# First norm of an MLA and differential-attention trunk: input split on arrival, root applied to the latents

## The reference

```python
def rmsnorm(x, g, eps=NORM_EPS):
    xf = x.astype(jnp.float32)
    y = xf * lax.rsqrt(jnp.mean(xf * xf, axis=-1, keepdims=True) + eps)
    return (y * g.astype(jnp.float32)).astype(x.dtype)

h = rmsnorm(x, g_attn_pre[0])
lat = h @ w_down                                   # 1024 x 704
c_q = rmsnorm(lat[..., :384], g_q_lat)
c_kv = rmsnorm(lat[..., 384:640], g_kv_lat)
k_pe = rope(lat[..., 640:], cos, sin)
q = c_q @ w_uq
kv = c_kv @ w_ukv
```

## Time and profile before

| what | value |
| --- | --- |
| median of 3 runs | 2650.4 us (2642.67 to 2661.89) |
| the profiled execution's own time | 2648.62 us |
| its span in the profile | 2646.8 us |
| mean granted TensorE clock | 0.975 |
| TensorE busy in the span | 2455.5 us (93%) |

### The profile page before, as it was taken

One profiled execution on the slowest core, in us unless ns is written; L12 is line 12 of the kernel. 1 busy time (PEld: TensorE's weight loads), 2 busy tenths in 40 slices (PEclk: granted clock), 3 DMA queues, 4 the chain that ended last, 5 costly groups with the idle time before them and its releaser, 6 DMA issues.

```text
span 2646.8 us, 31568 instructions
## 1 busy us (share of the span) xinstructions
PE 2455.5 (93%) x11940; PEld 1962.3 (74%) x11940; DVE 1928.3 (73%) x2189; ACT 847.8 (32%) x1439; POOL 1478.9 (56%) x1133
## 2 busy tenths in 40 slices
PE   7999999999999999996799899988989999999994
PEld 4788888777777777773577787766777777777772
DVE  4467664696887888889766677763796878888878
ACT  3245442342111111113346555652342111111112
POOL 4231113635888888884431323213636888888883
PEclk9999999999999999998999999988999999999997
DMA  3121215411111111113211212142311111111112
GB/s 136 48 70 66 80 56 209 142 56 40 49 64 48 48 49 55 50 40 152 64 50 47 64 49 92 37 159 111 135 56 40 62 51 48 48 51 53 56 58 109
DMA packets 51237, 191.98 MB, mean 73 GB/s; under 512 B 5904, under 2 KB 6416, under 8 KB 47376
## 3 DMA queue, kind: packets, MB, share of 16 engines
q1 hardware_dynamic: 39184, 148.92, 16.8%
q10 hardware_dynamic: 11904, 41.05, 4.1%
HBM read 146.43 MB, written 29.36 MB: 66 GB/s over the span
## 4 chain that ended last, share of the span: by engine, by line
PE 73%; DVE 16%; ACT 5%; issue 3%; DMA 2%; SPq 1%; ACTq 0%; POOL 0%; POOLq 0%; DVEq 0%
PE ps L1187 9%; PE ps L1188 9%; PE ps L1189 9%; PE ps L1209 6%; PE ps L1210 5%; PE ps L1211 5%; PE ps L1018 3%; PE ps L990 2%; PE ps L992 2%; PE ps L991 2%; PE ps L1055 2%; PE ps L1110 1%; PE ps L1035 1%; PE ps L1112 1%; PE ps L1111 1%
## 5 line engine op out<-in xcount | busy, mean ns | idle before, releaser
L2026 DVE TENSOR_TENSOR a<-a,ps 128x1024 f32<-128x1024 f32 x336 | 409.1, 1219 | 195.1 <-PE ps L1211 187.5
L739 POOL CAST w_hi<-w_raw 128x1024 fp32r<-128x1024 f32 x78 | 84.8, 1087 | 774.1 <-PE ps L992 272.4
L1209 PE MATMUL ps<-hid,ring 128*128 128x512 f32 x704 | 295.9, 420 | 26.5 <-DVE a L2026 13.2
L1545 ACT ACTIVATE cy<-cx,cv 128x1024 f32<-128x1024 f32 x76 | 94.8, 1247 | 674.0 <-DVE cx L1997 674.0
L821 POOL TENSOR_TENSOR ring<-w_raw,ring 128x512 fp32r<-128x512 f32 x206 | 298.8, 1450 | 16.5
L1210 PE MATMUL ps<-hid,ring 128*128 128x512 f32 x704 | 278.5, 396 | 0.0
L1211 PE MATMUL ps<-hid,ring 128*128 128x512 f32 x704 | 277.9, 395 | 0.0
L819 POOL CAST ring<-w_raw 128x512 fp32r<-128x512 f32 x206 | 168.2, 816 | 182.8 <-PE ps L1211 91.9
L1187 PE MATMUL ps<-h,ring 128*128 128x512 f32 x608 | 236.7, 389 | 0.0
L1188 PE MATMUL ps<-h,ring 128*128 128x512 f32 x608 | 236.7, 389 | 0.0
L1189 PE MATMUL ps<-h,ring 128*128 128x512 f32 x608 | 236.5, 389 | 0.0
(11 more groups left out here) (263 smaller groups left out, 6532.9 us busy)
## 6 DMA issues: line engine op xcount, KB each, us to landing
w_raw<-in_W SPq DMA_DIRECT2D x166, 512.0 KB, 3.2
raw_d<-in_W SPq DMA_DIRECT2D x44, 512.0 KB, 3.2
h<-o_dram ACTq DMA_DIRECT2D x2, 6144.0 KB, 20.7
x_dram<-x ACTq DMA_DIRECT2D x6, 2048.0 KB, 8.2
x<-x_dram SPq DMA_DIRECT2D x2, 4096.0 KB, 12.7
dsw<-draw SPq DMA_DIRECT2D x64, 128.0 KB, 2.3
o_dram<-most SPq DMA_DIRECT2D x6, 1024.0 KB, 4.0
o_dram<-dost SPq DMA_DIRECT2D x6, 1024.0 KB, 3.9
```

Of the source, the lines that this page charges most:

```text
L1209: pe.matmul(out, wh, xh, start=True, stop=False)
L2026: dve.tensor_tensor(a[:, f, :], a[:, f, :], src, ALU.add).then_inc(acc_done, 1)
```

## The change

- The four DMAs of the input's first half and the one of `par` change places in ACT's queue: `par` is first.
- In the first norm ACT rounds the input times its factor per channel straight into `h` (a Copy with the factor as its scale), then squares the input into a buffer of its own for each tile (`xs0`, `xs1`, `xs2`; no wait for TensorE). DVE computes input times factor minus the rounded part into `h` in one operation. The root is not in `h` any more.
- DVE adds the squares of k = 0 to 6 of each half, six additions, in PSUM bank 4; the last of them writes to SBUF. TensorE then sums a half with two matmuls by ones (`first_sums`): half 0 behind the first two turns of the first pair, half 1 behind its last turn. The 16 matmuls of `x_stats(0)` are gone.
- The root of each half is made by ACT from banks 6 and 7 into `rstd_0`. DVE multiplies each latent bank by it where it used to copy the bank.
- POOL has no part in the first norm.
- DVE's last three operations on lambda stand behind `latents()`.

```diff
--- before.py
+++ after.py
@@ -418,6 +418,8 @@
         assert off[0] <= base + 51 * SLOT + small_cols * 4
         cst = at("cst", 22, 1)
         lam_raw = nc.alloc_sbuf_tensor_at("lam_raw", [P, 256], F32, offset=base + 23 * SLOT)
+        xs0, xs1, xs2 = at("xs0", 38, 4), at("xs1", 42, 3), at("xs2", 28, 1)
+        rstd_0 = at("rstd_0", 45, 1)
         lam_mul = nc.alloc_sbuf_tensor_at("lam_mul", [P, 128], F32, offset=base + 24 * SLOT)
 
         ps = ctx.enter_context(nc.psum_tensor("ps", [P, 8 * HB], F32))
@@ -446,6 +448,7 @@
         a_sq, ss_add, a_stat, a_ln, a_rstd = (sem(n) for n in ("a_sq", "ss_add", "a_stat", "a_ln", "a_rstd"))
         a_normed, x_sq, x_stat, x_ln, x_rstd = (sem(n) for n in (
             "a_normed", "x_sq", "x_stat", "x_ln", "x_rstd"))
+        x0_hi, x0_lo, x0_add, x0_stat = (sem(n) for n in ("x0_hi", "x0_lo", "x0_add", "x0_stat"))
         f_new, b_kept, acc_first, xq_add, b_stat = (sem(n) for n in (
             "f_new", "b_kept", "acc_first", "xq_add", "b_stat"))
         h_f, h_hi = sem("h_f"), sem("h_hi")
@@ -487,7 +490,7 @@
         N_T = HEADS * NJ * (NJ + 1) // 2
         X_IN = {1: 16, 2: 32, 3: 48, 4: 64}
         SPILLED = {1: 16, 2: 32, 3: 48}
-        H_NO = {0: 0, 2: 1}
+        H_NO = {2: 0}
         X_NO = {2: 0, 4: 1}
 
         SQ0 = {"wo0": 0, "ffn0": 2 * KT - 1, "wo1": 3 * KT - 1, "ffn1": 5 * KT - 2}
@@ -552,6 +555,12 @@
         def added_bank(half):
 
             return bank((5, 1)[half])
+
+        def first_squares(half, k):
+
+            if half == 0:
+                return half_of(xs0, k // 2, k % 2)
+            return half_of(xs1, k // 2, k % 2) if k < 6 else half_of(xs2, 0, k - 6)
 
         def squares_of(half, k):
 
@@ -852,7 +861,6 @@
             pool.memset(ones[:, :], 1.0).then_inc(consts_ready, 1)
             for u in range(2):
                 split(u, u)
-            norm_help(0, sums=False)
             for u, free in enumerate(pairs_free(0, 0, by_half=True)):
                 split(u, 2 + u, free)
             with pool.Fori(2, LT // 2) as q:
@@ -895,8 +903,20 @@
                 pe.matmul(bank(6 + half), ones[:, :], squares_of(half, KT - 1), start=False, stop=True
                           ).then_inc(b_stat, 1)
 
+            def first_sums(half):
+
+                pe.wait_ge(x0_add, (KT - 2) * (half + 1))
+                pe.matmul(bank(6 + half), ones[:, :], first_squares(half, KT - 2), start=True, stop=False
+                          ).then_inc(x0_stat, 1)
+                pe.wait_ge(x_sq, KT * (half + 1))
+                pe.matmul(bank(6 + half), ones[:, :], first_squares(half, KT - 1), start=False, stop=True
+                          ).then_inc(x0_stat, 1)
+
             def wait_h(n, half, k):
-                wait_norm(pe, h_lo, H_NO[n], half * KT + k)
+                if n == 0:
+                    pe.wait_ge(x0_lo, half * KT + k + 1)
+                else:
+                    wait_norm(pe, h_lo, H_NO[n], half * KT + k)
 
             def pair_of_units(unit, ch, first_bank_use, norm, by_half=False, between=None):
 
@@ -930,7 +950,8 @@
                                   start=t == t0, stop=t == t1 - 1).then_inc(l_stat, 1)
 
             def latents():
-                pair_of_units(0, 0, True, 0, by_half=True)
+                pair_of_units(0, 0, True, 0, by_half=True, between=lambda: first_sums(0))
+                first_sums(1)
                 pair_of_units(2, 4, False, None)
 
                 pair_of_units(4, 8, False, None, between=lambda: latent_stats(0, QT, 4))
@@ -1223,7 +1244,6 @@
 
 
             pe.wait_ge(consts_ready, 1)
-            x_stats(0)
             latents()
 
             pe.wait_ge(consts_in, 16)
@@ -1263,21 +1283,31 @@
                 act.wait_ge(dn_done, down_count(layer, n - 2, KT - 1))
                 act.activation(cx[:, 2 * (n % 2), 0:HB], up_bank(n, "P1"), ACT.Copy).then_inc(bank_copied, 1)
 
-            def x_norm(n, first=False, spill=False):
+            def first_norm():
+
+                act.wait_ge(par_in, 16)
+                for i, (half, k) in enumerate(NORM_TILES):
+                    if k % 2 == 0:
+                        act.wait_ge(x_part[4 * half + k // 2], 16)
+                    act.activation(half_of(h, 2 * k, half), half_of(x, k, half), ACT.Copy, scale=gain("attn_pre0", k)
+                                   ).then_inc(x0_hi, 1)
+                    act.activation(first_squares(half, k), half_of(x, k, half), ACT.Square).then_inc(x_sq, 1)
+                for half in range(2):
+                    act.wait_ge(x0_stat, 2 * half + 2)
+                    rstd(half_of(rstd_0, 0, half), bank(6 + half), D, 0, x_ln, half + 1, x_rstd)
+
+            def x_norm(n, spill=False):
                 for step, i in NORM_STEPS:
                     if step == "L":
-                        act.wait_ge(x_stat, n // 2 * 16 + (i + 1) * KT)
+                        act.wait_ge(x_stat, (i + 1) * KT)
                         rstd(half_of(rstd_x, 0, i), bank(6 + i), D, 0, x_ln, 2 * n + i + 1, x_rstd)
                         continue
                     half, k = NORM_TILES[i]
                     if step == "A":
-                        if first:
-                            act.wait_ge(x_part[4 * half + k // 2], 16)
-                        else:
-                            wait_norm(act, x_new, X_NO[n], i)
+                        wait_norm(act, x_new, X_NO[n], i)
                         if i >= 2:
 
-                            act.wait_ge(x_stat, n // 2 * 16 + i - 1)
+                            act.wait_ge(x_stat, i - 1)
                         act.activation(half_of(sq, 0, i % 2), half_of(x, k, half), ACT.Square).then_inc(x_sq, 1)
                         if spill and k == KT - 1:
 
@@ -1619,8 +1649,8 @@
                     act.dma_start(x[:, 2 * g:2 * g + 2, half * HB:(half + 1) * HB],
                                   x_first[:, 2 * g:2 * g + 2, half * HB:(half + 1) * HB]).then_inc(x_part[4 * half + g], 16)
 
+            act.dma_start(par[:, :], small).then_inc(par_in, 16)
             load_x(0)
-            act.dma_start(par[:, :], small).then_inc(par_in, 16)
             load_x(1)
             act.dma_start(ident[:, :], consts[:, 0:128]).then_inc(consts_in, 16)
             act.dma_start(cst[:, 0, 0:512], consts[:, 128:640]).then_inc(mask_in, 16)
@@ -1633,7 +1663,7 @@
             act.wait_ge(eps_set, 2)
 
             act.preload_act_table_set("natural_log_exp_and_others")
-            x_norm(0, first=True)
+            first_norm()
 
             act.wait_ge(lam_step, 2)
             act.activation(lamb[:, 2:4], lamb[:, 0:2], ACT.Exp).then_inc(lam_exp, 1)
@@ -1661,6 +1691,26 @@
 
         @block.vector
         def _(dve):
+            def first_norm():
+
+                def add_square(i):
+                    half, k = NORM_TILES[i]
+                    if not 1 <= k <= KT - 2:
+                        return
+                    dve.wait_ge(x_sq, i + 1)
+                    dve.wait_ge(x0_add, (KT - 2) * half + k - 1)
+                    dve.tensor_tensor(first_squares(half, k) if k == KT - 2 else bank(4),
+                                      first_squares(half, 0) if k == 1 else bank(4), first_squares(half, k), ALU.add
+                                      ).then_inc(x0_add, 1)
+
+                for i, (half, k) in enumerate(NORM_TILES):
+                    dve.wait_ge(x0_hi, i + 1)
+                    dve.scalar_tensor_tensor(half_of(h, 2 * k + 1, half), half_of(x, k, half), gain("attn_pre0", k),
+                                             half_of(h, 2 * k, half).bitcast(F32), ALU.mult, ALU.subtract
+                                             ).then_inc(x0_lo, 1)
+                    if i:
+                        add_square(i - 1)
+
             def x_norm(n, post=None, pre=None, heads=True):
                 if n > 0:
 
@@ -1706,7 +1756,10 @@
                 def copies(q, turns):
                     for n, (u, half) in turns:
                         dve.wait_ge(proj_done, 4 * q + n + 1)
-                        dve.tensor_copy(half_of(lat, 2 * q + u, half), bank(n)).then_inc(proj_out, 1)
+                        if q == 0 and u == 0:
+                            dve.wait_ge(x_rstd, half + 1)
+                        dve.tensor_tensor(half_of(lat, 2 * q + u, half), bank(n), half_of(rstd_0, 0, half), ALU.mult
+                                          ).then_inc(proj_out, 1)
 
                 def norm(w, t0, t1):
                     dve.wait_ge(l_rstd, 2 * w + 2)
@@ -2091,7 +2144,7 @@
             dve.memset(eps[:, 0:1], NORM_EPS).then_inc(eps_set, 1)
             dve.memset(eps[:, 1:2], SUBLN_EPS).then_inc(eps_set, 1)
             dve.wait_ge(par_in, 16)
-            x_norm(0, None, "attn_pre0")
+            first_norm()
             dve.wait_ge(mask_in, 16)
             dve.tensor_copy(mask_q[:, :], cst[:, 0, 0:256]).then_inc(mask_ready, 1)
             dve.tensor_copy(mask_k[:, :], cst[:, 0, 256:512]).then_inc(mask_ready, 1)
@@ -2103,13 +2156,13 @@
```

(2 more changed lines are left out.)

## The result

The changed kernel takes 2634.32 us in the median (2633.05 to 2639.42, 7 runs), the kernel before 2650.40 (2642.67 to 2661.89, 7 runs). The two medians lie 16.1 us apart. The ratio of the runs is 0.9941, 95% interval 0.9930 to 0.9952, and that is 15.6 us less, where 18.6 had been forecast. The profiled execution's span fell from 2646.8 to 2631.1 us.

What follows compares the result with a forecast made beforehand. TensorE, busy in 93% of the span, was taken as the bound. -19.1 for the second pair's start plus 0.45 for lambda gave -18.6: 2630.0 profiled, 2631.8 as median, range 2619 to 2645.

Steps and rivals of the forecast that it cites:

- The sum: Whole kernel: -19.1 for the second pair's earlier start plus 0.45 for the moved lambda operations, -18.6 us.
- start of the second pair: TensorE's second pair of units in the first 125 us: starts at 44.5 instead of 63.6, 19.1 us sooner.
- lambda behind the latents: VectorE's moved lambda operations lie on the path while TensorE waits for L1768: +0.45 us, bounds nothing to 0.6.
- slower first matmul: Last tile before the second pair in the kernel before: about 0.3 us added for its first matmul.
- pair of sums by ones: TensorE's two fp32 matmuls summing a half's squares: 0.79 us each, 1.6 for two.
- ACT's price with a factor: First norm on ACT: a rounding with a factor per channel as its scale takes 0.72 us.
- VectorE's pace: First norm on VectorE: subtraction plus addition cost 1.27 us a tile, more than ACT's 1.16, so VectorE sets the pace.
- the 1.5 us kept as the other end: VectorE's first addition of a half, reading two SBUF buffers: taken as 0.69 us, with +1.5 as its other bound.
- The roots' new waits: VectorE's first and third bank copies wait for ACT's roots; the third starts at 45.9, with 8.8 us to spare.
- Rival C: TensorE over the whole span: granted clock one hundredth lower costs 25.2 us, giving 2657; chance 0.04.
- Rival B: Behind the second pair's start: something at a fixed time, a load, gives the lead back, giving 2650; chance 0.05.
- free as long as the tiles come slower: TensorE's first turn at its slow level: three matmuls cost 1.31 us, tiles come every 1.27, so almost nothing lost.

Runs made afterwards that it cites:

- b1: Changed kernel with lambda's last three VectorE operations back in front of the latents, ACT's Exp still behind both roots: 2639.70 us, ratio 0.9956 to the kernel before.
- a1: The changed kernel run again without any edit: 2635.13 us, ratio 0.9945 to the kernel before.
- a2: Kernel before with only the squares changed: own buffers, added on VectorE in PSUM, two matmuls by ones per half: 2650.99 us, ratio 1.0002.
- a3: Changed kernel with lambda's three VectorE operations between the first pair's copies of both halves, ACT's Exp between the roots: 2633.50 us, ratio 0.9939 to before.
- a4: Changed kernel with 18 small matmuls of ones on TensorE ahead of the first tile: 2631.66 us, ratio 0.9933 to the kernel before.
- b2: Changed kernel with, per half, all roundings before the squares on ACT and all subtractions before the additions on VectorE: 2631.57 us, ratio 0.9931 to before.
- b3: Changed kernel with the edits of b2, a4 and a3 together: 2630.49 us, ratio 0.9922 to the kernel before.
- b4: b3 with six DMAs moved from ACT's queue to SP's behind the first split, and 22 small matmuls from program start: 2625.64 us, ratio 0.9906 to before.

## Why the prediction came out as it did

The sum named two stretches, and the traces give each of them:

| step | forecast | measured |
| --- | --- | --- |
| start of the second pair, as the shift of its first bank | -19.1 | -18.35 |
| lambda behind the latents | +0.45 | +0.43 |
| shift at L1768's counterpart | -18.6 | -17.9 |
| shift at the end of the two traces | -18.6 | -15.7 |
| shift of the medians, from the ratio | -18.6 | -15.6 (-12.7 to -18.6) |

**The first 0.7 us** are sizes, of terms of the sum. The second pair of the kernel before started at 63.45 (L916 in TensorE's order of time) and not at 63.6: I had put 0.3 on its last tile for a slower first matmul, where the row (57.19 to 57.53) gives 0.1 over the usual 0.227. In the changed kernel it started at 44.64 and not at 44.5; ACT's first rounding was 0.2 late. And the first matmul behind each pair of sums by ones is followed after 0.64 us (44.64 to 45.28) where others are after 0.23. The first of these two steps of 0.4 was made up for, as each pair of sums took 1.3 us in place of 1.6; the second lies behind the start of the second pair, where the sum had no term for it. So that start moved by 18.8 us, and the first bank behind it by 18.35.

**ACT's price with a factor** was 0.72, by the row with such operands, and **VectorE's pace** 1.26 for 1.27. The addition of two SBUF buffers took 0.70 with POOL idle, so the 0.69 was right and the 1.5 us kept as the other end were not needed. The roots' new waits cost nothing: the third copy waited for the root until 46.70 (forecast 45.9; ACT began the root only 0.6 us after TensorE had gone on to the next matmul) and was needed some 8 us later, and a bank left with its root in 0.69, as fast as a copy. b1 shows how narrow the reason was: with lambda's wait in front, the same wait on ACT holds TensorE.

**The other 2.2 us** could be traced to no step of the change. The code behind L1768 is the same in all these kernels, and the time that it takes is not. One profiled execution each:

| kernel | first bank of the second pair | L1768's counterpart | from there to the end | of that, MLA attention | mean granted clock |
| --- | --- | --- | --- | --- | --- |
| before | 69.09 | 123.05 | 2523.8 | 247.5 | 0.975 |
| changed | 50.74 | 105.13 | 2526.0 | 247.8 | 0.975 |
| a1 | 51.32 | 105.72 | 2528.4 | 250.9 | 0.972 |
| a2 | 67.55 | 121.51 | 2528.4 | 249.8 | 0.972 |
| a3 | 51.11 | 105.08 | 2527.6 | 249.9 | 0.971 |
| a4 | 50.37 | 104.76 | 2527.2 | 250.5 | 0.972 |
| b1 | 55.99 | 109.95 | 2527.8 | 251.4 | 0.973 |
| b2 | 48.94 | 103.34 | 2529.0 | 250.1 | 0.971 |
| b3 | 47.79 | 101.76 | 2522.4 | 246.7 | 0.976 |
| b4 | 45.16 | 99.13 | 2525.2 | 246.9 | 0.974 |

The fourth column spreads over 6.6 us and does not turn with the change: a2, which shifts the work by 1.5 us only, lies 4.6 above the trace of before, and b3, which shifts it by 21, lies 1.4 below.

Between before and changed, 1.7 of the 2.2 us lie in the first FFN. VectorE's first row there is at 552.50 in before and at 534.85 in the changed kernel, 17.65 sooner; the first row behind it is at 1236.95 and at 1220.96, 15.99 sooner. So this stretch took 684.5 us before and 686.1 in the changed kernel, and in the other eight traces it took 684.0 to 685.6: 685.4 in a1, which is the changed kernel again, and 684.5 in b2. That is scatter from one execution to the next, and the first pair of traces happened to have most of its width between them.

The medians say the same. Set against the kernel before of its own group, each kernel's median fell by between 1.9 us less and 1.7 us more than its landmark moved, 0.7 less on average over the nine. Whether a constant loss of that size is real stays open: the interval of the ratio holds both 15.6 and 17.9.

Rival C's mechanism is real in part. Over the ten traces a lower mean clock goes with a longer rest: 0.971 and 2529.0 in b2, 0.976 and 2522.4 in b3, some 13 us for a hundredth, about half of the 25.2 at which the prediction priced it. But it does not turn with the change, and it does not explain the first pair, whose mean clocks are both 0.975.

**Rival B**, a lead that is given back, did not occur: 17.9 of 18.35 us are there at 105, 17.65 at 535, and what is missing further on lies within the spread of the ten traces.

The Trainium skill ("TensorE: Matmul & The Clock Gate", What's actually happening) gives the throttled state as the default that activity releases. The traces agree: 0.43 a matmul until 20.85 in the changed kernel's first turn, 0.23 from the second matmul on in a4. What the prediction had right is that this is free as long as the tiles come slower, and b3 shows the price, 2.1 us, when they do not.

## What to carry to other kernels

A norm in front of a product need not stand in front of it: the factor per channel can go in while the input is split, and the root per token multiplies the result where it leaves its bank, which costs nothing when the bank is copied anyway (0.69 us either way here). Then price the start by three paces, that of the tiles, that of TensorE at its slow level and that of the queue that issues the first DMAs; the slowest hides the others, and taking them off one after another (b2 to b4, with lambda's 0.4 among it) gave 6.0 us more at the landmark and 8.7 in the median. Compare small gains at landmarks a few us behind the change, since 2500 us of unchanged code spread by 6.6 us from one execution to the next.

## What had not been expected

- The clock column need not show the slow level at the program's start. Over the stretch in which matmuls stand 0.43 us apart, the changed kernel's table by stretch gives a granted clock of 1.00:

```profile
16.00:20.80 4.80, 4.78 (x11) 3.79 (x12) 4.24 (x7) 4.80 (x10) 0.00 (x0) 1.00 1.06 380
```

  The distance of starts is the better witness there: 0.43 us at the 1.2 GHz level, 0.23 at 2.4 GHz. Where the level falls again after matmuls at the high one the column does follow: it gives 0.50 in b4 from 11.7 to 14.0.
- One subtraction of VectorE with two SBUF operands took 2.86 us beside a subtraction of POOL with two SBUF operands (b4), and 0.75 alone: nearly four times, and 2 us on the path. With the slow matmuls that followed it cost 4.6.
- A matmul that follows fp32 sums by ones is followed after 0.64 us in place of 0.23, once for each change.
- ACT's 15 DMA issues and its table load ended between 13.9 and 15.0 us in the changed kernel and a1 to b3, though their number is the same; the issue for the identity took some 2.2 to 2.6 us where the one for `par` took 0.4. In a2, where `par` comes fifth, these two took 1.84 and 0.61.
